# Four latent-attention query groups with ScalarE-crossed rope columns, and another order of the recurrent block's last down groups

## The reference, cut to what matters

```
# MLA: 8 heads, 128 plain and 64 rotated columns each
q = (cq @ w_uq).reshape(bsz, seq, MLA_HEADS, QK_NOPE + QK_ROPE)
q_nope, q_pe = q[..., :QK_NOPE], _rope(q[..., QK_NOPE:], cos, sin)
def _rope(x, cos, sin):                 # x1, x2: first and second 32 of the 64 columns
    return concatenate([x1 * c - x2 * s, x1 * s + x2 * c])
s = (qn @ k_nope + qp @ k_pe) * scale;  p = softmax(masked s);  o = p @ v

# recurrent block, then the second attention's keys and values
y = hs * silu(g);   x = x + gate * (y @ w_out)
h = rmsnorm(x, kv_norm_g) * (1 + scale) + shift
k, v = split(h @ w_kv)
```

## Time and profile before

| | us |
|---|---|
| median of three runs | 807.93 |
| the profiled execution, whole | 808.98 |
| its span, first to last instruction | 806.7 |
| TensorE busy with matmuls | 780.2 |
| VectorE busy | 596.8 |
| ScalarE busy | 405.3 |

### The profile page before, as it was taken

How to read it: one execution, slowest core, us unless ns; L and a number is a source line. 1 busy time by engine, 2 the same in 40 slices (tenths; PEclk the granted TensorE clock), 3 DMA queues, 4 the chain that set the end, 5 groups by cost and what they waited for, 6 DMA issues and landing times.

```text
span 806.7 us, 12491 instructions
## 1 busy us (share of the span) xinstructions
PE 780.2 (97%) x5198; PEld 712.5 (88%) x5198; DVE 596.8 (74%) x788; ACT 405.3 (50%) x493; POOL 29.6 (4%) x58
## 2 busy tenths in 40 slices
PE   8999999999999999999999999999799988999996
PEld 7999898998899899778998899988799868999985
DVE  4886888877686797679888777766789876656643
ACT  5455235544443435554445444444678966645631
POOL 0000000000000010000000000001300004000000
PEclk9999999999999999999999999999999999999998
DMA  8877438897687622356589887765134642754101
GB/s 327 321 277 260 170 140 321 340 347 270 254 312 283 239 88 99 122 179 248 185 305 348 326 309 279 272 241 203 56 128 151 234 164 105 264 206 158 53 27 52
DMA packets 26695, 174.72 MB, mean 217 GB/s; under 512 B 2960, under 2 KB 3344, under 8 KB 7568
## 3 DMA queue, kind: packets, MB, share of 16 engines
q1 hardware_dynamic: 26640, 173.93, 59.3%
HBM read 172.87 MB, written 1.05 MB: 216 GB/s over the span
## 4 chain that ended last, share of the span: by engine, by line
PE 86%; DVE 6%; ACT 4%; issue 1%; DMA 1%; POOL 0%; SPq 0%; DVEq 0%; POOLq 0%; ACTq 0%
PE bank L503 11%; PE bank L504 11%; PE bank L505 11%; PE Y L588 10%; PE Y L590 10%; PE Y L587 10%; PE bank L529 2%; PE bank L531 2%; PE bank L530 2%; PE bank L881 2%; DVE w_low L1375 2%; PE bank L883 2%; PE bank L882 2%; PE bank L652 1%; PE bank L550 1%
## 5 line engine op out<-in xcount | busy, mean ns | idle before, releaser
L1375 DVE TENSOR_TENSOR w_low<-raw,w_high 128x2048 fp32r<-128x2048 f32 (+2 forms) x129 | 285.3, 2220 | 63.9 <-ACT w_high L993 61.4
L993 ACT CAST w_high<-raw 128x2048 fp32r<-128x2048 f32 (+2 forms) x129 | 238.0, 1853 | 88.4 <-DMA raw<-weights 75.7
L503 PE MATMUL bank<-xT_h,w_high 128*128 128x256 f32 x736 | 208.8, 284 | 0.0
L504 PE MATMUL bank<-xT_l,w_high 128*128 128x256 f32 x736 | 208.4, 283 | 0.0
L505 PE MATMUL bank<-xT_h,w_low 128*128 128x256 f32 x736 | 208.3, 283 | 0.0
L503 PEld LDWEIGHTS bank<-xT_h,w_high 128*128 128x128 f32 x736 | 141.2, 192 | 1.5 <-issue 0.2
L504 PEld LDWEIGHTS bank<-xT_l,w_high 128*128 128x128 f32 x736 | 141.2, 192 | 1.0
L505 PEld LDWEIGHTS bank<-xT_h,w_low 128*128 128x128 f32 x736 | 141.2, 192 | 0.0
L587 PE MATMUL Y<-w_high,hT_h 128*128 128x512 f32 x324 | 129.2, 399 | 4.5 <-DVE hT_l L1391 2.6
L588 PE MATMUL Y<-w_low,hT_h 128*128 128x512 f32 x324 | 129.5, 400 | 0.0
L590 PE MATMUL Y<-w_high,hT_l 128*128 128x512 f32 x324 | 103.3, 400 | 0.0
(11 more groups left out here) (238 smaller groups left out, 1202.5 us busy)
## 6 DMA issues: line engine op xcount, KB each, us to landing
raw<-weights SPq DMA_DIRECT2D x149, 1024.0 KB, 5.1
rows<-rows_in SPq DMA_DIRECT2D x9, 512.0 KB, 8.0
raw<-weights SPq DMA_DIRECT2D x7, 512.0 KB, 5.2
raw<-weights SPq DMA_DIRECT2D x4, 768.0 KB, 4.3
raw<-weights SPq DMA_DIRECT2D x2, 896.0 KB, 4.5
x<-x_in SPq DMA_DIRECT2D x2, 512.0 KB, 5.1
kT<-rows_in SPq DMA_DIRECT2D x2, 512.0 KB, 9.2
out<-x SPq DMA_DIRECT2D x4, 256.0 KB, 2.1
```

The source lines that it names most:

```text
L503: mm(dst, high, xh[:, kt, :], start=kt == 0, stop=False)
L504: mm(dst, high, xl[:, kt, :], start=False, stop=False)
L993: nc.scalar.copy(w_high[:, n % RING, start:COLS[n]], raw[:, s % RAW, start:COLS[n]]).then_inc(w_high_ready, 1)
L1375: tt(w_low[:, n % RING, start:COLS[n]], slot[:, start:COLS[n]], f32(w_high[:, n % RING, start:COLS[n]]), ALU.subtract).then_inc(raw_done, 1)
```

## The change

In MLA a piece of group g loses the fourth tile (1152 columns for 1536) and `qp` is projected before `qn`. ScalarE copies the rope tile from PSUM to `area[:, 7]` in four copies of 32 partitions with neighbouring 32s exchanged, and VectorE's `rope` waits for them. ScalarE's list of a group becomes: exponentials, the four crossed copies, PT copies, scaled copy of `qn`, outputs' high parts, weight split. The wait for value banks moves from the first scores to the first value products. In the recurrent block the down groups run as (1,0), (2,0), (1,1), (3,0), (2,1), (3,1), then block 0's transposes, and block 1's transposes run between the two halves of `moba_values(0, 1)`. One weight split of ScalarE moves ahead of `conv_high(3)`, and one of VectorE's moves behind block 0's gated residual and the wait for its root.

```
-        add("mla", "q", g, 2 * GT * QT * P)
+        add("mla", "q", g, (GT + 1) * QT * P)
-    attention("mla", ("qn", "qp"))
+    attention("mla", ("qp", "qn"))
+RG_TAIL = [(1, 0), (2, 0), (1, 1), (3, 0), (2, 1), (3, 1)]
@@ TensorE, values(): ahead of the products
+                    for b, n in ((0, 1), (1, 0), (1, 1)) if (phase, h) == ("mla", 0) else ():
+                        await_evacuated(pe, "mla", "v", b, n)
@@ TensorE, project(g)
-                for i, kind in enumerate(("qn", "qp")):
-                    up(PI["mla", "q", g], ("mla", kind, g), GT * i, QT, hT_h, hT_l)
+                n, dst = PI["mla", "q", g], open_unit("mla", "qp", g)
+                await_piece(n)
+                in_order("mla", "qp", g)
+                up_tile(dst[:, 0:SEQ], n, GT, QT, hT_h, hT_l).then_inc(product, 1)
+                up(n, ("mla", "qn", g), 0, QT, hT_h, hT_l)
@@ TensorE, await_q(g)
-                    for b, n in ((0, 1), (1, 0), (1, 1)):
-                        await_evacuated(pe, "mla", "v", b, n)
@@ TensorE, recurrent tail
-            tail("rg", early=lambda: rs2kv_transposes(0))
-            for n in range(2):
-                moba_values(0, n)
-            rs2kv_transposes(1)
+            for g, b in RG_TAIL:
+                down("rg", g, b)
+            rs2kv_transposes(0)
+            moba_values(0, 0)
+            moba_values(0, 1, lambda: rs2kv_transposes(1))   # called ahead of its second half
@@ ScalarE
+            def crossed(g):
+                await_product(act, "mla", "qp", g)
+                if g:
+                    act.wait_ge(rope_ready, g)
+                for i in range(P // 32):
+                    to, source = slice(32 * i, 32 * i + 32), slice(32 * (i ^ 1), 32 * (i ^ 1) + 32)
+                    last = nc.scalar.copy(area[to, 7, :], bank_of("mla", "qp", g)[source, 0:SEQ])
+                last.then_inc(crossed_ready, 1)
@@ ScalarE, loop over g
                 if g < MXG:
+                    crossed(g)
+                if g:
+                    transposed_high("mla", heads)
+                if g < MXG:
                     await_product(act, "mla", "qn", g)
...
-                    transposed_high("mla", heads)
+                    outputs_high("mla", heads)
                 split_ahead(("mla", "q", 3), g)
-                if g:
-                    outputs_high("mla", heads)
@@ ScalarE, recurrent loop, ahead of conv_high(i + 1)
+                if i == 2:
+                    split_ahead(("rg", "g", 3), 0)
@@ VectorE, rope(g)
-                await_product(dve, *key)
+                dve.wait_ge(crossed_ready, g + 1)
...
-                stt(out=area[:, 6, :], in0=src[:, SEQ:], scalar=scale, in1=sinT, ...).then_inc(evacuates(*key), 1)
-                await_evacuated(dve, *key)
+                link(stt(out=area[:, 6, :], in0=area[:, 7, :], scalar=scale, in1=sinT, ...))
@@ VectorE, recurrent tail
+            split_ahead(("rg", "down", 3), 1)
+            gated_residual("rg", 0, 0)
+            await_rstd("rs2", 0)
             split_ahead(("rg", "down", 3), 2)
-            gated_residual("rg", 0, 0)
@@ host, piece_of
-        ... + [a, b, c, d, b, a, d, c], axis=1), QT)
+        ... + [a, b, c, d], axis=1), QT)
```

More of the change, by code:

```diff
@@ L183, in down_table @@
         t.extend((phase, g, b) for g in range(groups - TAIL[phase]) for b in range(TB))
-        t.extend((phase, g, b) for b in range(TB) for g in range(groups - TAIL[phase], groups))
+        if phase == "rg":
+            t.extend((phase, g, b) for g, b in RG_TAIL)
+        else:
+            t.extend((phase, g, b) for b in range(TB) for g in range(groups - TAIL[phase], groups))
     return t
@@ L195, in last_unit @@
     if phase == "mla" and kind == "q":
-        return ("mla", "qp", n)
+        return ("mla", "qn", n)
     return {"uk": ("mla", "k", 3), "uv": ("mla", "v", 1, 1),
@@ L343, in build @@
         kpe_ready, lora_ready, lora_high, lora_low, rope_ready = sem("kpe_ready"), sem("lora_ready"), sem("lora_high"), sem("lora_low"), sem("rope_ready")
+        crossed_ready = sem("crossed_ready")
         u_ready, conv_ready, uc_high, uc_low = sem("u_ready"), sem("conv_ready"), sem("uc_high"), sem("uc_low")
@@ L850, in rs2kv_transposes, with moba_values @@
                 transposes("rs2kv", z, blocks=[b], z_name="rs2")
-            def moba_values(b, n):
+            def moba_values(b, n, between=lambda: None):
                 dst = open_unit("mo", "v", b, n)
                 for i in range(2):
+                    if i:
+                        between()
                     await_piece(PI["mo", "v", 2 * n + i])
@@ L1675, in rope @@
                 key = ("mla", "qp", g)
-                await_product(dve, *key)
+                dve.wait_ge(crossed_ready, g + 1)
                 src = bank_of(*key)
                 scale = float(NOPE + ROPE) ** -0.5
-                stt(out=area[:, 5, :], in0=src[:, 0:SEQ], scalar=scale, in1=cosT, op0=ALU.mult, op1=ALU.mult)
-                stt(out=area[:, 6, :], in0=src[:, SEQ:], scalar=scale, in1=sinT, op0=ALU.mult, op1=ALU.mult).then_inc(evacuates(*key), 1)
-                await_evacuated(dve, *key)
+                stt(out=area[:, 5, :], in0=src[:, 0:SEQ], scalar=scale, in1=cosT, op0=ALU.mult, op1=ALU.mult).then_inc(evacuates(*key), 1)
+                link(stt(out=area[:, 6, :], in0=area[:, 7, :], scalar=scale, in1=sinT, op0=ALU.mult, op1=ALU.mult))
                 tt(area[:, g, :], area[:, 5, :], area[:, 6, :], ALU.add).then_inc(rope_ready, 1)
@@ L1892, in piece_of @@
         (a, b), (c, d) = [(uq[:, h, NOPE:NOPE + ROPE // 2], uq[:, h, NOPE + ROPE // 2:]) for h in heads]
-        return tiles(np.concatenate([uq[:, h, 0:NOPE] for h in heads] + [a, b, c, d, b, a, d, c], axis=1), QT)
+        return tiles(np.concatenate([uq[:, h, 0:NOPE] for h in heads] + [a, b, c, d], axis=1), QT)
     if kind == "ax":
```

## The result

The changed kernel takes 802.01 us (median of 4 runs, 801.54 to 803.28), the kernel before 808.2 on the same chip (807.61 to 809.98): a ratio of 0.9926 with an interval of 0.9911 to 0.9941, so 6.0 us less (4.8 to 7.2). The forecast was 800.0, the range 797.5 to 804.0. A second build of the same source gave 801.42 and 0.9901 (0.9881 to 0.9921) later on. The profiled execution of the first spans 801.0 us (before: 806.7), that of the second 798.7.

A forecast was written before the change was run, and what follows sets the result against it. The prediction took TensorE's work plus a few waits to bound the kernel. MLA's 2.1 + 1.8 - 1.0 = 2.9 us and the tail's 5.0 sum to 7.9, so 807.93 - 7.9 = 800.0 us, range 797.5 to 804.0.

The forecast's parts named there:

- First scores: MLA group 0: the wait before the scores goes and fewer matmuls run, 1.05 + 1.08 = 2.1 us gained.
- Groups 1 to 3: MLA: each group gains 0.6 us, not the 1.08 of removed matmuls; three groups give 1.8 us.
- X: MLA, time from the end of the scores to the first value product: falls from 5.47 to 4.88 us.
- PT copies straight behind crossed copies: Sign that the forecast is right: ScalarE's order in three MLA groups, with X near 4.9.
- Behind group 3: End of MLA: ScalarE's later weight split delays the layer norm's transposes; TensorE loses about 1.0 us.
- The tail: Recurrent block: reordering gains 2.4 us at block 0's values and 2.6 at block 1's, 5.0 in all.
- the root: GpSimd's root for block 0 in the recurrent tail: the added wait keeps it at 0.30, against 1.50 for block 1.
- (a): Rival, chance 0.12: the clock falls after the new idle time at 660; 1.65 us back, 801.7.
- (b): Rival, chance 0.07: crossed copies in MLA cost 0.59 each; MLA gives -0.7 us, time 803.6.
- (c): Rival, chance 0.08: keys' pieces set the pace behind block 1, the tail's gain is given back; 805.0.
- (d): Rival, chance 0.03: gaps ahead of value products bring TensorE's lower clock in attention; slower, up to about 830.
- The sum: Whole kernel: MLA 2.9 plus tail 5.0 gives 7.9 us less.

The follow-up runs named there:

- pt_copies_first: The changed kernel with ScalarE's PT copies queued ahead of the exchanged copies; 809.75 us, ratio 1.0015 to the kernel before.
- one_straight_copy: The changed kernel with one straight 128-partition copy in place of the four exchanged ones, which alters the output; 799.07 us, ratio 0.9881.
- queries_on_vector: The changed kernel with the scaled copy of `qn` on VectorE, ahead of rope, instead of ScalarE; 799.14 us, ratio 0.9876.
- last_split_back: The changed kernel with ScalarE's last MLA weight split ahead of the outputs' high parts again, as before the change; 801.0 us, ratio 0.9893.
- rg_only: The kernel before with only the recurrent part of the change; 803.13 us, ratio 0.9931.
- after_again: The second build of the changed kernel, nothing edited, timed later; 801.42 us, ratio 0.9901.
- mla_only: The changed kernel with the recurrent tail and both moved weight splits as before, so only the MLA part stays; 806.67 us, ratio 0.9975.
- combined: The changed kernel with the edits of last_split_back and queries_on_vector, plus 18 thrown-away matmuls ahead of block 0's values; 799.24 us, ratio 0.9875.

## Why the prediction was right, and where it was not

**First scores: right.** 2.1 forecast, 2.1 to 2.3 measured: by the timelines it takes 8.94 from the first `up` matmul of the group to the scores (312.42 to 321.36) instead of 11.24 (312.51 to 323.75); the chain, which puts the scores at 321.52, makes it 2.1. TensorE came at 321.4 to 321.5, the forecast said 321.6.

**Groups 1 to 3: the step that failed.** Forecast 0.6 each, 1.8 in all; measured 0.22 in all. Two things were wrong in it. The first is the price of the copies in the term X. "Four take 1.3" was read from a pair of 128-partition casts of 0.66 that overlap; the four exchanged ones take 1.49 and start every 0.38, so they don't overlap. With a start 0.1 later than forecast that puts the PT copy at +4.55 instead of +4.25, and X, forecast 4.88, is 5.1 to 5.2 (before 5.4 to 5.5): 0.3 gained, not 0.6. The second is that the list of what can be late left out the banks and so put at nothing what lies between the first value product and the next scores. The second product now waits nearly 0.2 for the copy of `qn`, which had been out of the way before and stands behind the PT copies, and that much is given back in each group. "PT copies straight behind crossed copies" came true and accounts for X; rope's first instruction, which frees the first product's bank, happens to end with the PT copy. pt_copies_first shows that the bank holds the product, one_straight_copy what the copies cost (9.49 to 9.05 a group with 1.1 less of copies), queries_on_vector the nearly 0.2.

**Behind group 3: right.** 1.0 forecast, 1.04 measured for block 1 and 0.84 for block 0, and last_split_back takes it away.

**The tail: right in mechanism and size.** 5.0 forecast, 5.1 measured in rg_only and after_again. A wait of 0.36 to 0.55 before (3,0) stands in the traces whose early down group ran at the full clock, since TensorE got there sooner, and in no other (it was forecast at nothing); the root stayed at 0.30. GpSimd's timeline of the changed kernel, as in the earlier trace rows:

```profile
655.00 0.30 POOL L944 TENSOR_SCALAR small<-small 128x1 f32<-128x1 f32 x1 [83.10 <-ACT z L1041]
...
664.39 1.50 POOL L944 TENSOR_SCALAR small<-small 128x1 f32<-128x1 f32 x1 [8.45 <-ACT z L1041]
```

**The rivals.** (a), the lower clock after the new idle time, was given 0.12 and came in 3 of 8 traces; the first profile is one of them. In it a drop elsewhere was absent (early down group 14.86 instead of 15.81), which hid most of its price: 4.0 of the tail's 5.1 were left. The price was 1.5, forecast 1.65. The sentence that the two waits of the trace before agree with a count that differs between executions could not be read from one trace, and its row for the second wait ends at 680.00, ahead of that wait's end; the stretch behind it, 680 to 690, is at 1.00 too. What shows the difference is 13.86 against 12.37 us for the same source. (b): the copies cost 0.37 to 0.38, not 0.59. (c) is out: from block 1's transposes to the end all traces take 130.2 to 130.4, so nothing is given back. (d): the granted clock in attention is 1.00 in the changed kernel, with waits of 0.7; pt_copies_first, with waits of 2.61, is where (d)'s mechanism shows.

**The sum.** By the traces it is 1.3 to 1.5 (attention) + 5.1 (tail) = 6.4 to 6.6 without the drop, against 7.9. The measured 6.0 us (4.8 to 7.2) and the second build's 8.0 (6.4 to 9.6) lie on both sides of it. The forecast time, 800.0, was 2.0 us below the first build and 1.4 below the second; the one term that was wrong in every trace is the 1.8 of groups 1 to 3. The range held. That the second build's 8.0 is so near to the forecast 7.9 is luck: some 1.4 us of the 7.9 did not come, and its trace makes them up ahead of the first scores, which start 3.7 us sooner than before, 2.1 to 2.3 of them by the edit.

## What to carry to other kernels

When an edit changes the order in which PSUM units are opened or freed, list for every later unit whose bank it takes and which engine frees that, and at what place in that engine's queue. A product can have all its inputs and still wait for its output's former owner. And where TensorE stands idle for a couple of microseconds, give the lower clock behind it a chance and a price of its own, read from a stretch at either level, instead of a yes or no.

## What the runs showed of the hardware that I had not expected

*Copies with exchanged partitions.* Four ScalarE copies of 32 partitions by 256 columns out of PSUM take 1.49 us, 0.37 to 0.38 from start to start; one straight copy of 128 partitions and 256 columns takes 0.37. A quarter of the partitions costs the same, and these copies don't overlap, while pairs of 128-partition operations do (0.66 for two casts of 256 columns in the earlier trace rows, 0.86 for two copies of 384 here, one of which takes 0.48). No run separates the 32 partitions from the exchange.

*GpSimd beside VectorE.* 0.30 against 1.50 us for the same instruction, the longer one beside a VectorE split that reads two SBUF operands, in the kernel before and after alike. The Trainium skill (SBUF — State Buffer, "SBUF: two separate sides") says that a VectorE operation with two SBUF inputs and a GpSimd operation that reads SBUF exclude each other at a port pair that they share; the traces agree: in both kernels the long instruction ends 0.16 us behind the split (664.39 + 1.50 and 663.44 + 2.29 in the changed one).

*The lower clock behind a wait.* Waits of TensorE of 2.5 to 2.7 us were followed by the lower level in all three traces ahead of (3,0) in the old order, in all three groups of pt_copies_first, in 3 of 8 traces ahead of block 0's values, and in neither of the two traces that have such a wait ahead of block 1's values (before, mla_only). The same length has both outcomes, by place and by execution.

*Where an execution starts.* The first projection matmul starts at 11.43 in the trace of before, 10.97 and 10.83 in the two of the changed kernel, 10.17 in queries_on_vector's and 9.54 in combined's, though nothing was changed there. The first transposes, which wait for the load of x, start at 8.22, 7.76 and 7.62 in the first three, and eight of them take 1.97 us in the first two, against 0.95 at 377.38. By the first scores the two traces of one source are 1.3 us apart, though they start 0.14 apart. So two spans can differ by a microsecond or more without a reason in the edit, and terms below that have to be read from intervals inside the traces, as above. Even there a stretch that nobody touched can differ: from the layer norm's transposes to the first early down group it takes 239.51 to 239.69 us in twelve traces and 238.24 in two.
